# Two rebuilt attentions in a fused transformer kernel, with the softmax weights multiplied in on GpSimd

## The reference, cut to what matters

```
h = rmsnorm(x);  q, k, v.., z = split(h @ w_in);  x = x + (attention * silu(z)) @ w_out
```

```
A: causal, window 128; one extra logit ("sink") for each head in the sum of the softmax
B: o = g0 * o_cmp + g1 * o_slc + g2 * o_win,   g = sigmoid(gates)
   o_cmp: attention to 15 compressed keys (a small MLP over blocks of 32 keys)
   o_slc: attention to the selected blocks (with 256 tokens all of them are selected: causal)
   o_win: window 512, so causal as well, with keys and values of its own
```

## Time and profile before

| | |
|---|---|
| median of 3 runs | 2685.07 us (2680.35 to 2687.39) |
| the profiled execution's own time | 2685.55 us |
| its span | 2683.7 us |
| PE busy | 2525.0 us (94%) |
| DVE, ACT, POOL busy | 1363.9 us (51%), 1154.1 us (43%), 68.5 us (3%) |
| attention A until `a_out` starts | 1808.1 to 1989.6 us |
| `a_out` | 1989.6 to 2083.1 us |
| `b_att` | 2083.1 to 2267.1 us |
| attention B until `b_out` starts | 2267.1 to 2581.4 us |
| `b_out` | 2581.4 to 2671.6 us |

### The profile page before, as it was taken

The page is one execution under the profiler, slowest core; times in us unless marked ns, Lnnn a source line. Parts: engine busy times, 40 slices in busy tenths (PEclk is TensorE's granted clock), DMA queues, the critical chain, the costliest instruction groups (busy, mean ns, idle before and its releaser), DMA issues.

```text
span 2683.7 us, 32482 instructions
## 1 busy us (share of the span) xinstructions
PE 2525.0 (94%) x12004; PEld 1970.2 (73%) x12004; DVE 1363.9 (51%) x2129; ACT 1154.1 (43%) x1829; POOL 68.5 (3%) x95
## 2 busy tenths in 40 slices
PE   4699999999899989999999999999989999999998
PEld 1377886666666668888888888777778877877776
DVE  0144445666444455555555555654555464545554
ACT  1245444444333354443444344544544454544543
POOL 1000000000000000000000000000000000000000
PEclk9699999999899989999999999999999999888999
DMA  9954665676688855555555555552235674111133
GB/s 340 330 172 158 192 198 171 239 250 223 220 305 291 299 202 188 187 189 188 188 186 189 188 188 177 184 188 94 79 124 188 221 236 142 48 63 47 63 112 123
DMA packets 243163, 494.18 MB, mean 184 GB/s; under 512 B 7928, under 2 KB 8288, under 8 KB 241808
## 3 DMA queue, kind: packets, MB, share of 16 engines
q1 hardware_dynamic: 239232, 476.08, 53.2%
q0 software_dynamic: 3536, 16.94, 1.9%
q10 hardware_dynamic: 320, 0.13, 0.0%
HBM read 491.02 MB, written 2.10 MB: 184 GB/s over the span
## 4 chain that ended last, share of the span: by engine, by line
PE 70%; issue 16%; DMA 6%; DVE 4%; ACT 3%; POOL 0%; SPq 0%; ACTq 0%; DVEq 0%; POOLq 0%
PE acc L1389 19%; PE acc L1391 18%; PE acc L1390 18%; PE acc L1684 4%; DMA raw<-in_w_mod 3%; PE aux L1706 3%; DMA raw<-in_w_in 2%; PE turn L1694 2%; PE acc L1413 2%; ACT whi L483 1%; PE turn L1435 1%; PE aux L1413 1%; DVE wlo L854 1%; DMA raw<-in_w_o 1%; PE aux L1816 1%
## 5 line engine op out<-in xcount | busy, mean ns | idle before, releaser
L854 DVE TENSOR_TENSOR wlo<-raw,whi 128x1024 fp32r<-128x1024 f32 x712 | 864.2, 1226 | 845.3 <-ACT whi L483 841.7
L483 ACT ACTIVATE whi<-raw 128x1024 fp32r<-128x1024 f32 x712 | 743.9, 1058 | 979.5 <-PE acc L1391 822.8
L1389 PE MATMUL acc<-whi,xhi 128*128 128x512 f32 x2176 | 882.9, 406 | 11.9 <-DVE wlo L854 6.2
L1391 PE MATMUL acc<-whi,xlo 128*128 128x512 f32 x2176 | 859.7, 395 | 0.0
L1390 PE MATMUL acc<-wlo,xhi 128*128 128x512 f32 x2176 | 859.3, 395 | 0.0
L1389 PEld LDWEIGHTS acc<-whi,xhi 128*128 128x128 f32 x2176 | 416.1, 191 | 135.1 <-issue 46.0
L1391 PEld LDWEIGHTS acc<-whi,xlo 128*128 128x128 f32 x2176 | 415.3, 191 | 90.3
L1390 PEld LDWEIGHTS acc<-wlo,xhi 128*128 128x128 f32 x2176 | 416.5, 191 | 79.7
L1389 PE MATMUL acc<-whi,hhi 128*128 128x512 f32 x512 | 201.1, 393 | 2.0 <-DVE hlo L880 2.0
L1391 PE MATMUL acc<-whi,hlo 128*128 128x512 f32 x512 | 199.4, 389 | 0.0
L1390 PE MATMUL acc<-wlo,hhi 128*128 128x512 f32 x512 | 199.3, 389 | 0.0
(11 more groups left out here) (272 smaller groups left out, 1891.7 us busy)
## 6 DMA issues: line engine op xcount, KB each, us to landing
raw<-in_w_ff SPq DMA_DIRECT2D x128, 1024.0 KB, 5.2
raw<-in_w_mod SPq DMA_DIRECT2D x96, 1024.0 KB, 5.2
raw<-in_w_in SPq DMA_DIRECT2D x80, 1024.0 KB, 5.4
raw<-in_b_w_in SPq DMA_DIRECT2D x48, 1024.0 KB, 5.0
raw<-in_a_w_in SPq DMA_DIRECT2D x36, 1024.0 KB, 5.0
raw<-in_w_o SPq DMA_DIRECT2D x16, 1024.0 KB, 7.5
raw<-in_a_w_out SPq DMA_DIRECT2D x16, 1024.0 KB, 5.1
raw<-in_b_w_out SPq DMA_DIRECT2D x16, 1024.0 KB, 5.0
```

Of the source, the lines that this page charges most:

```text
L483: act.activation(whi[:, k % 2, on], raw[:, n % 4, on], ACT.Copy).then_inc(hi_ready, 1)
L854: dve.tensor_tensor(wlo[:, k % 2, on], raw[:, LOAD_OF_UNIT[k] % 4, on], whi[:, k % 2, on].bitcast(F32), ALU.subtract)\
L1389: pe.matmul(bank, hi[:, kt, tok], w_hi, start=kt == k_first, stop=False, skip_group_check=True)
L1391: mm = pe.matmul(bank, lo[:, kt, tok], w_hi, start=False, stop=kt == k_first + UK * k_units - 1, skip_group_check=True)
```

## The change

- **Layout of the output.** The gate z is computed transposed: `multiply_gate` has the weights as the stationary operand and 256 tokens moving, 12 matmuls of 256 columns for a tile where there were 6 of 512. Attention's outputs are computed transposed too: the 64 values of a head are the stationary operand, and the turned weights move. The gated output goes straight into `ghi`/`glo`; the 32 transposes and 8 builds of `a_o` and of `b_o` go away.
- **Slots instead of rounds.** The loops over g are unrolled into 16 slots in A and 32 in B (`slots` 2 and 4 for each (g, t)). A slot has four items: in A four heads, in B two heads in the two kinds slc and win. Heads lie in pairs on partitions 0-63 and 64-127, so `scores` goes in turn over the two halves of PE's rows, and `outputs` over the two halves of its columns. The compressed kind is done once for each round for all 8 heads (matmuls of 30 columns, one transpose, 4 matmuls with a widened value matrix).
- **Fill.** Each slot has two half units of weights before its other work in A and one in B. 38 half units are spread over each attention: the 16 units of z and the first 3 units of the output projection, whose order of units (`OUT_ORDER`) is changed so that these don't need the last group of heads.
- **Softmax.** The maximum comes out negated (min of -x), the sink is an extra column of the exponentials, written by POOL. The exponentials are multiplied by 1/sum (times the gate g1 or g2 in B) before they are turned. **This multiplication is one POOL instruction for each slot**, on 4 x 128 or 4 x 256 elements for each of 128 partitions. DVE makes the 4 reciprocals for it. PE's `turn_probs` waits for it (`weighed`).
- **Queries and keys** are turned during `a_in` and `b_att` in blocks of 8 transposes of 128 x 128, and no longer inside the loop; `a_in` computes k and v first. POOL's copies of queries, keys and values go away.

```diff
@@ gpsimd
+        def weigh(at, q):
+            keys = (q // at["slots"] % T + 1) * P
+            x = at["prob"][q % 2].rearrange("p (k n) -> p k n", k=4)[:, :, 0:keys]
+            pool.wait_ge(weight_ready, at["slot0"] + q + 1)
+            pool.tensor_tensor(x, x, s8[:, q % 2, 0:4].unsqueeze(2).to_broadcast([P, 4, keys]), ALU.mult).then_inc(weighed, 1)
...
@@ vector
+            for q in range(ns + 4):
+                n, i = divmod(q, slots)
+                if q < ns and n % T == 1 and i == 0:
+                    half_gate(n // T)
+                if q < ns:
+                    maxima(q)
+                if i == 3 % slots and n >= 3 // slots + 1:
+                    outputs_low(n - 3 // slots - 1)
+                if 1 <= q <= ns:
+                    weigh(q - 1)
+                if q < ns and n % T == 1 and i == 1:
+                    gate(n // T)
+                if i == 2 % slots and n >= 2 // slots + 1:
+                    outputs(n - 2 // slots - 1)
+                if name == "b" and i == 0 and n < ROUNDS:
+                    compressed_maxima(n)
...
+                if name == "b" and i == 1 and n < ROUNDS:
+                    compressed_weights(n)
+                if q < ns:
+                    split_halves(first + 8 + at["halves"] * q, at["halves"])
...
+                if 1 <= q <= ns:
+                    copy_probs(q - 1)
...
@@ tensor
+        def multiply_gate(u, k, tiles):
+            for kk in tiles:
+                if kk % 2 == 0:
+                    pe.wait_ge(lo_ready, 2 * u + 1 + kk // 2)
+                kt = UK * k + kk
+                for c in range(4):
+                    bank = acc[:, 2 + c // 2, c % 2 * L:(c % 2 + 1) * L]
+                    cols = slice(c * P, (c + 1) * P)
+                    pe.matmul(bank, whi[:, u % 2, kk, cols], xhi[:, kt, :], start=kt == 0 and c % 2 == 0, stop=False,
+                              skip_group_check=True)
...
+            def scores(q):
...
+                    pe.wait_ge(topped, 4 * (s0 + q))
+                for u in range(2):
+                    j = 2 * i + u if name == "a" else i
+                    for c in range(2):
+                        on = slice(c * HD, (c + 1) * HD)
+                        mm = pe.matmul(acc[:, c, u * keys:(u + 1) * keys], at["qT"][on, g, t, j, :],
+                                       at["kT"][u][on, g * L:g * L + keys], start=True, stop=True)
+                mm.then_inc(scored, 1)
...
+            def turn_probs(q):
+                t = q // slots % T
+                prob = items(at["prob"][q % 2], (t + 1) * P)
+                pe.wait_ge(weighed, s0 + q + 1)
...
+            def outputs(q):
...
+                        for c in range(2):
+                            mm = pe.matmul(aux[c * HD:(c + 1) * HD, n % 2, to:to + w], at["v"](g, u, k),
+                                           pT[:, 512 * c + o:512 * c + o + w], start=i == k == u == 0, stop=k == t,
+                                           tile_position=(0, c * HD), skip_group_check=True)
...
+            for q in range(ns):
+                n, i = divmod(q, slots)
+                new_gate = n % T == 1 and i == 0
+                if new_gate:
+                    outputs_of(q - 2)
+                for half in range(at["halves"]):
+                    fill(4 + at["halves"] * q + half)
+                if q + 1 < ns:
+                    scores(q + 1)
+                if q >= 2 and not new_gate:
+                    outputs_of(q - 2)
+                if q >= 1:
+                    turn_probs(q - 1)
+                if name == "b" and i == slots - 1:
+                    compressed(n)
+            fill(36)
+            outputs_of(ns - 2)
+            turn_probs(ns - 1)
+            fill(37)
+            outputs_of(ns - 1)
...
-        with pe.Fori(0, KVG) as g:
-            fill = filler("a_z", g)
-            queries(0, g, fill)
-            pe.wait_ge(values_ready, g + 1)
-            v_of = lambda k: v_g[:, 0, k]
-            rounds(ROUND_A, [(n * P, n - 1, kTs[:, bass.ds(g * L, n * P)], v_of) for n in (1, 2)], g, sm_a,
-                   fill)
-        pe.wait_ge(gated, KVG)
...
+        attention("a")
```

More of the change, by code:

```diff
@@ L757, in gate @@
[L757 to L773 removed]
+                scaled(kv_a, banks(0), ACT.Copy, norm).then_inc(acc_freed, 1)
+            else:
+                scaled(q2[:, :, (g - 1) * NW:g * NW], banks(g), ACT.Copy, norm_q).then_inc(acc_freed, 1)
@@ new lines, in add_output @@
+        def add_output(name, n):
+            part = res3[:, :, n * NW:(n + 1) * NW]
+            dve.tensor_tensor(part, banks(GROUP[name] + n), part, ALU.add).then_inc(acc_freed, 1)
+        dve.wait_ge(masks_in, 16)
+        attention("a")
+        for i in range(3, 16):
+            split(UNIT["a_out"] + i + 2, 1)
+            for g in NEXT_ROWS.get(i, ()):
+                build(BUILD["b"] + g, 2 * g, xhi, xlo, norm_b)
+            if i in OUT_DONE:
+                group_done(UNIT["a_out"] + i)
+                add_output("a_out", OUT_DONE[i])
@@ L1318, in step @@
                 ins.then_inc(blk_ready, 1)
-                if n == 0:
-                    twice(1)
+                twice(keys_of(n + 1))
+            elif kind == "turn" and n == "b_ks":
+                dve.wait_ge(flat_turned, FLAT[n] + 1)
+                twice(keys_of(4))
+            elif kind == "norm":
+                spread_norm(ATTN["b"])
             elif kind == "hidden":
@@ L1679, in scores @@
-        def scores(r, g, per, p, kind):
-            keys, t, kT, _ = kind
-            apart(pe, masked2, 4 + plus(4 * r + p - 1, 4 * per, g), pe_passed)
-            for h in range(2):
-                mm = pe.matmul(acc[:, p % 2, h * L:h * L + keys], qT[:, 2 * p + h, t, :], kT, start=True, stop=True)
-            mm.then_inc(scores2, 1)
-        def turn_probs(r, g, per, p, kind, sm):
-            kt, n = -(-kind[0] // P), min(kind[0], P)
-            pe.wait_ge(exp2, plus(4 * r + p + 1, 4 * per, g))
-            for h in range(2):
-                for k in range(kt):
-                    o = (h * kt + k) * P
-                    mm = pe.transpose(turn[0:n, p % 2, o:o + P], sm[r % 2][2 * p + h][:, k * P:k * P + n], ident[:, :])
-            mm.then_inc(probs_turned, 1)
@@ L1697, in outputs @@
-        def outputs(r, g, per, p, kind):
-            keys, _, _, v_of = kind
-            kt, n = -(-keys // P), min(keys, P)
-            apart(pe, probsT_ready[p % 2], plus(2 * r + p // 2 + 1, 2 * per, g), pe_passed)
-            for h in range(2):
-                for k in range(kt):
-                    o = (h * kt + k) * P
-                    hh = 2 * p + h
-                    mm = pe.matmul(aux[:, r % 2, hh * HD:(hh + 1) * HD], pT[0:n, p % 2, o:o + P], v_of(k),
-                                   start=k == 0, stop=k == kt - 1)
-            mm.then_inc(out2, 1)
@@ L1745, in filler @@
-        def filler(name, g):
-            done = [0]
-            def fill(part, n):
-                for _ in range(FILLS[name][part][n]):
-                    k, kk = divmod(done[0], UK)
-                    done[0] += 1
-                    if k == 0 and kk == 0:
-                        pe.wait_ge(acc_freed, plus(GROUP[name], 1, g))
-                    multiply(UNIT[name] + k, k, 4, 2, i=g, per=4, tiles=(kk,))
-            return fill
-        pe.wait_ge(roped, 1)
-        turn_keys(kv_a, 0)
@@ new lines, in output @@
+        def output(name, i):
+            n, k = OUT_ORDER[i]
+            if k == 3:
+                pe.wait_ge(gated, ATTN[name[0]]["round0"] + ROUNDS)
+            if k == 0 and n >= 2:
+                pe.wait_ge(acc_freed, GROUP[name] + n - 1)
+            multiply_out(name, i)
+        attention("a")
+        through = lambda g: pe.wait_ge(acc_freed, GROUP["a_out"] + g // 2 + 1)
+        for i in range(3, 16):
+            output("a_out", i)
+            if i in NEXT_ROWS:
+                turn_rows("b", res3, NEXT_ROWS[i], ready=through)
```

811 lines of the change are left out of this document (438 added, 373 removed).

## The result

| | before | after |
|---|---|---|
| median, 4 runs each | 2686.23 us (2680.35 to 2689.28) | 2533.55 us (2531.68 to 2535.98) |
| profiled execution, its span | 2685.55, 2683.7 us | 2531.68, 2529.7 us |

What follows compares the result with a forecast made beforehand. PE was taken to set the time; savings of 36 us (A and `a_out`) and 91 us (B and `b_out`), net of added turns, cut the 2683.7 us span to 2556.7, about 2558 us; range 2525 to 2612.

Steps and rivals of the forecast that it cites:

- Fill, scores, outputs, turns: PE's items per slot: half unit 2.88 us, scores 0.6 or 1.05, outputs 0.55 or 1.0, turns 0.45 or 0.85.
- that rival: Scores and outputs in both attentions: the array's halves run one behind the other, 79 us less 10, 2627 us; chance 5%.
- Start and end of the stages: Around the slots: start 14, end 10 and 13 output units 71 us for B; 13.3, 8.3 and 71 for A.
- P and the circle: POOL's product P, 2.1 or 1.2 us; the DVE-POOL-PE chain of 6.0 or 3.8 us lies under PE's 6.6 or 5.3.
- POOL becomes the bound: Rival in B: POOL's product takes 4.2 and 2.3 us, adding 33 and 10 us, 2601 us; chance 17%.
- POOL held, 10 us: B's t = 1 slots: DVE's subtraction makes POOL wait, +0.65 us for each of 16 slots, 10 us.
- Clock, 10 us in B and 3 in A: Allowance for PE's granted clock staying below full: 10 us in B, taken at 0.95, and 3 in A.
- New gates and low part, 5 us in B: B: waits for DVE's gate instruction before new gates' first fills, 4 us, and the low part written before weights, 1 us.
- the gates' 4 us: A: DVE's gate instruction must end before a new gate's first fill, four times about 1 us, 4 us.
- `b_att`, +3.5 us: Stage ahead of the last attention: three turns of queries and a norm add 3.5 us.
- the one called better: Rival: POOL isn't held and the clock is full, 21 us off the forecast, 2537 us; chance 12%.
- the forecast itself: Whole kernel: about 2558 us, the case from 2545 to 2575 us; chance 47%.

Runs made afterwards that it cites:

- same_half: Changed kernel with both matmuls of each pair in scores and outputs put on the first half of the array; 2585.37 us, 0.9634 of the kernel before.
- weigh_twice: Changed kernel with GpSimd multiplying each slot's exponentials by their weights twice, one after the other; 2598.25 us, 0.9676 of the kernel before.
- before_no_cmp: Kernel before, with the compressed branch of the last attention left out and the fills spread over the other four kinds; 2613.16 us, ratio 0.9730.
- early_zero_norm: Changed kernel with VectorE's zeroing, head pattern and spreading of norms moved earlier, ahead of the last attention; 2522.10 us, 0.9392 of the kernel before.
- early_weigh: Changed kernel with VectorE working out a slot's weights at the end of that slot, not during the next; 2529.96 us, 0.9422 of the kernel before.

## Why the prediction was right, and where its sizes were off

*Fill, scores, outputs, turns.* Scores, outputs and turns are right to some hundredths of a microsecond, each (0.65, 1.06, 0.59, 1.02; turns of eight 0.85), and a fill with its changes of work is 3.04 for 3.08. Of a group's 47.9 us, PE is idle 0.8, and 47.1 is work, where the forecast has 47.6. `same_half` shows the reason given, the halves at once, as well as what that rival should have priced: 52 us, not 79 - 10.

*Start and end of the stages.* 14.2, 9.7 and 70.9 us for B (14, 10, 71). `a_out` and `b_out` begin without idle time.

*P and the circle.* 1.90 and 1.04 for 2.1 and 1.2; the twice of the copy was a guess, and a near one. The circle does lie under PE's slot: PE waits 3.7 us in B. `weigh_twice` shows that the rival "POOL becomes the bound" had the right order of size for B: 43 us were priced, at 4.2 and 2.3 us, and 49 came at 3.8 and 2.1. It had nothing for A, where 13 came, and nothing for the clock.

*POOL held, 10 us.* The first term that was mis-sized. Of B's t = 1 slots only one in four has a held product (2.81 us), beside the gate's instruction of 1024 elements (L1244), not a subtraction, and PE waits behind such a product only once, 0.2 us at 2423.8. The subtraction (L889) does come in the middle of a product, as forecast, but in one slot of four: it starts 1.1 us into the product of 2338.47.

```profile
2339.56 1.88 DVE L889 TENSOR_TENSOR wlo<-raw,whi 128x1024 fp32r<-128x1024 f32 x1 [1.17 <-ACT whi L500]
```

There the subtraction is held (1.88 us for 1.22) and the product is not (1.89). The forecast took from the earlier trace rows that POOL is the one that waits; there the subtraction had started first. So how often they meet and who pays were both wrong. Most of the 3.7 us of waits for POOL, 2.7, stand in the slot of each group where DVE writes the low part (`outputs_low`) ahead of the weights, a term that had 1 us.

*Clock, 10 us in B and 3 in A.* The second: it measured 0 in both, the clock is 1.00. The reason given, that the stretches of tiny matmuls leave, fits `before_no_cmp`; the forecast took only a part of it.

*New gates and low part, 5 us in B.* A group's 47.9 us are 0.3 more than 4 x (5.3 + 6.6), so it measured about 1, and PE's rows name 0.4 us of waiting for `half_gate`. In A the gates' 4 us were right in size (without them a group would be 33.2 of the 34.17), but by luck: PE's rows name only 1.6 us of waiting for `half_gate` there, and 3.0 for the copies of the turned weights (L1281), since the outputs are taken ahead of the fill where a new gate begins.

These terms, 10 + 10 + 5, are nearly the whole of B's 26.4 us; the slots without them, 190 forecast, are the 188.8 of the window with its waits. A's 6 us are the clock's 3 and small pieces at its ends.

*`b_att`, +3.5 us.* The step that failed: only PE's own new work was counted, not what it would wait for. It measured +14.4; two of DVE's small preparations stood behind subtractions that are paced by PE itself. The forecast's rule, to count what is queued ahead of each new producer, was applied to the attentions and not to the stage ahead.

So the case that came is the one called better (12%, 2537 us): not held, full clock. The 2533.6 lie below the forecast itself, 2545 to 2575, which had 47%. That the better case's number is so near is luck in part: it takes off 21 us, where its three terms are 23, it has none of the 11 that `b_att` took back, and none of the smaller pieces that went the other way; without the 11 the time is the 2522 of `early_zero_norm`. Of the whole gain of 153 us only the halves' 52 are measured by themselves. What the fill across the stages' edges and the new layout of the outputs gave each was not taken apart.

## What to carry to other kernels

An operation moved to GpSimd to relieve VectorE can be paid for there too: compare VectorE's busy time with and without it, not only GpSimd's. Whether it is depends on what VectorE does beside it (1347.0 us in one order, 1328.5 in another, 1328.1 without the products). Ask of each new wait of TensorE where its producer stands in its engine's queue, in the stages around the change as well; two small instructions behind a block of paced work cost 11 us here, more than the choice of engine for the products (3 us), and a product one step too early in VectorE's queue cost 27. And price a stall on TensorE above its own length: in `weigh_twice` 30.5 us more of waits in B came with 18.7 us more at a lower clock.

## What the runs showed of the hardware

VectorE pays for GpSimd's products, much of it in tiny instructions. DVE's timeline around the product of 2302.11 to 2303.15 us in the changed kernel, and the groups of one line in the changed kernel and in the run without products:

```profile
2301.95 0.27 DVE L1316 TENSOR_REDUCE silu_c<-qkv 128x8 f32<-128x120 f32 x1
2302.26 0.92 DVE L1317 TENSOR_SCALAR silu_c<-silu_c 128x8 f32<-128x8 f32 x1
2303.22 0.20 DVE L1318 RECIPROCAL silu_c<-silu_c 128x8 f32<-128x8 f32 x1
```

```profile
L1317 DVE TENSOR_SCALAR silu_c<-silu_c 128x8 f32<-128x8 f32 x8 | 9.5, 1186 | 0.3
```

```profile
L1316 DVE TENSOR_SCALAR silu_c<-silu_c 128x8 f32<-128x8 f32 x8 | 1.4, 171 | 0.3
```

Eight elements take 1186 ns on average in place of 171; the one shown, 0.92 us, ends 0.03 us after POOL's product. The reductions beside a product (L1316, 0.27 us) keep their time. In A it is subtractions that are held, one of 2.02 us for 1.22 beside a product of 2.78 at 1846.67, and in B some too (1.88, shown above). Over the span DVE's busy time is 1347.0 us with the products and 1328.1 without them; two lines of tiny instructions (L1317 and L1309) make 12 us of the difference, subtractions the most of the rest. With the weights at the end of the slot it is 1328.5 (`early_weigh`). In the kernel before the subtraction kept its time and POOL's copy was longer; here both directions occur. The Trainium skill, "SBUF — State Buffer", section "SBUF: two separate sides", calls the shared pair of ports an exclusive lock that whichever engine starts first holds for its whole instruction; these rows agree, down to the instruction of eight elements: the gate's instruction that started before the product holds it (2.81 us for 1.90), and the product that started before the subtraction holds that.

The two halves of the array need not be asked for in alternation. With all of one half first, eight records overlap as well as before (0.66 us) and sixteen lose more than half of the gain (1.51, between 1.02 and 1.89). In the sixteen at 2302.03 single records start 0.11 us apart at both ends of the run and 0.05 apart only from 2302.51 to 2302.90, so the halves overlap in its middle alone.
